# A hybrid S5 and GLA decoder layer: one over the root of every norm as exp(-ln/2) on ScalarE, in place of a mean and a reciprocal on VectorE and a square root between them

## The reference

```python
def rmsnorm(x, g):
    return x * lax.rsqrt(jnp.mean(x * x, axis=-1, keepdims=True) + EPS) * g

h = rmsnorm(x, g_mix);  z = h @ w_in          # u | q | k | v | r | a_low | gate_s5 | gate_gla
# S5: 32 groups, complex diagonal state x_t = A x_{t-1} + B u_t, y = Re(C x) + D u
z5 = gelu(y5);  o5 = z5 * sigmoid(z5 @ w_s5_glu)
# GLA: 4 heads, S_t = diag(alpha_t) S_{t-1} + k_t^T v_t, o_t = q_t S_t
og = og * lax.rsqrt(jnp.mean(og * og, axis=-1, keepdims=True) + EPS) * g_gla_norm    # per head, 128 wide
og = og * silu(r)
x = x + (sigmoid(gate_s5) * (o5 @ w_s5_br) + sigmoid(gate_gla) * (og @ w_gla_br)) @ w_out
x = x + jnp.square(relu(rmsnorm(x, g_ffn) @ w_ff1)) @ w_ff2
y = rmsnorm(x, g_final)
```

## Time and profile before

| | us |
|---|---|
| median of three runs | 3229.48 |
| lowest and highest | 3226.78 and 3229.75 |
| the profiled execution | 3223.25 |
| its span | 3221.4 |
| PE busy | 3006.3 (93%) |
| VectorE busy | 1452.4 (45%) |
| ScalarE busy | 505.0 (16%) |

### The profile page before, as it was taken

One profiled execution on the slowest core, in us unless ns is written; L12 is line 12 of the kernel. 1 busy time (PEld: TensorE's weight loads), 2 busy tenths in 40 slices (PEclk: granted clock), 3 DMA queues, 4 the chain that ended last, 5 costly groups with the idle time before them and its releaser, 6 DMA issues.

```text
span 3221.4 us, 46813 instructions
## 1 busy us (share of the span) xinstructions
PE 3006.3 (93%) x19116; PEld 2906.8 (90%) x19116; DVE 1452.4 (45%) x2573; ACT 505.0 (16%) x671; POOL 1161.5 (36%) x917
## 2 busy tenths in 40 slices
PE   4999997788999999999999999778999999999996
PEld 4899986688999999999999999667999999999996
DVE  7744536546353333333573353565445333333335
ACT  3221222141110000000122221213211000000001
POOL 3423321134444444444443323112444444443441
PEclk9989988899999999999999999788999999999998
DMA  3322323243111111111213222234121111111111
GB/s 123 103 93 67 74 83 91 85 150 92 47 43 47 49 44 49 44 49 47 96 51 115 66 68 67 86 97 165 60 76 44 49 47 47 46 46 47 46 46 68
DMA packets 115472, 226.59 MB, mean 70 GB/s; under 512 B 11824, under 2 KB 37200, under 8 KB 114128
## 3 DMA queue, kind: packets, MB, share of 16 engines
q1 hardware_dynamic: 65664, 119.57, 12.4%
q10 hardware_dynamic: 49616, 104.15, 10.0%
HBM read 181.71 MB, written 41.96 MB: 69 GB/s over the span
## 4 chain that ended last, share of the span: by engine, by line
PE 88%; DVE 8%; ACT 1%; issue 1%; DVEq 1%; DMA 1%; ACTq 1%
PE ps L456 27%; PE ps L457 26%; PE ps L458 26%; PE ps L598 2%; DVE f_g L1762 2%; DVE f_h L1353 1%; DVE r_o L1353 1%; PE ps L657 1%; PE ps L655 1%; DVE f_m L1353 1%; PE ps L677 1%; PE ps L678 1%; PE ps L692 1%; DVE f_o L1353 1%; DVE r_h L1353 1%
## 5 line engine op out<-in xcount | busy, mean ns | idle before, releaser
L438 POOL TENSOR_TENSOR w_hi<-w_raw,zero 128x512 fp32r<-128x512 f32 x456 | 524.2, 1150 | 1944.3 <-PE ps L458 1934.4
L456 PE MATMUL ps<-r_h,w_hi 128*128 128x344 f32 (+1 forms) x2736 | 896.9, 328 | 37.0 <-DVE r_h L1353 12.3
L458 PE MATMUL ps<-r_h,w_lo 128*128 128x344 f32 (+1 forms) x2736 | 881.7, 322 | 0.0
L457 PE MATMUL ps<-r_o,w_hi 128*128 128x352 f32 (+1 forms) x2280 | 736.7, 323 | 0.0
L440 POOL TENSOR_TENSOR w_lo<-w_raw,w_hi 128x512 fp32r<-128x512 f32 x456 | 640.0, 1403 | 64.7
L456 PE MATMUL ps<-r_z,w_hi 128*128 128x344 f32 (+1 forms) x1776 | 588.7, 331 | 27.1 <-DVE f_h L1353 15.6
L457 PE MATMUL ps<-r_h,w_hi 128*128 128x344 f32 (+1 forms) x1800 | 583.1, 324 | 0.0
L458 PE MATMUL ps<-r_z,w_lo 128*128 128x344 f32 (+1 forms) x1776 | 576.1, 324 | 0.0
L456 PEld LDWEIGHTS ps<-r_h,w_hi 128*128 128x128 f32 x2736 | 519.8, 190 | 49.7 <-issue 24.0
L458 PEld LDWEIGHTS ps<-r_h,w_lo 128*128 128x128 f32 x2736 | 519.6, 190 | 0.0
L457 PE MATMUL ps<-r_m,w_hi 128*128 128x344 f32 (+1 forms) x1392 | 448.2, 322 | 0.0
(11 more groups left out here) (336 smaller groups left out, 2860.2 us busy)
## 6 DMA issues: line engine op xcount, KB each, us to landing
w_raw<-wpack SPq DMA_DIRECT2D x456, 256.0 KB, 2.6
f_z<-s_constants ACTq DMA_DIRECT2D x16, 514.0 KB, 3.6
f_h<-s_constants ACTq DMA_DIRECT2D x16, 514.0 KB, 3.6
f_h<-xT ACTq DMA_DIRECT2D x4, 1040.0 KB, 9.5
gate_s_scratch<-f_o ACTq DMA_DIRECT2D x8, 520.0 KB, 3.3
f_h<-gate_s_scratch ACTq DMA_DIRECT2D x8, 520.0 KB, 14.1
f_h<-xT ACTq DMA_DIRECT2D x8, 520.0 KB, 3.5
f_o<-xT ACTq DMA_DIRECT2D x4, 1040.0 KB, 9.9
```

What stands on the lines that cost most here:

```text
L438: pool.tensor_tensor(w_hi[:, s, :], raw, zero[:, :].to_broadcast([P, WB]), ALU.subtract)
L456: pe.matmul(out, wh, h, start=first, stop=False)
L457: pe.matmul(out, wh, l, start=False, stop=False)
L458: return pe.matmul(out, wl, h, start=False, stop=last)
```

## The change

Every norm's root changes its form. Before: VectorE makes mean plus EPS from PSUM, ScalarE takes the square root, VectorE the reciprocal. After: ScalarE reads the sums from PSUM with Ln, with 1/n as the scale and a tile `eps` as the bias, and then takes Exp with scale -0.5 in place; VectorE waits for the result and scales. So PSUM is freed by ScalarE where it was freed by VectorE. The Ln of a head's part stands at the end of ScalarE's round in which PE makes the sum, behind the gate blocks; Exp follows the second Ln. Heads 2 and 3 have their sums a round earlier (6 and 8), all heads are scaled one round earlier against their sums, the small sample norm's Ln and Exp stand in round 0. The constant tile is set by VectorE before the tile of ones, and ScalarE waits for that before its first Exp.

```diff
-SAMPLE_MEAN = 1
-NORM_SUM = [1, 3, 7, 9]
+SAMPLE_SCALE = 2
+NORM_SUM = [1, 3, 6, 8]
...
+        eps = sb("eps", [P, 1])
...
             def norm_root(n, at):
-                act.wait_ge(ms_read, 3 * (n + 1))
-                act.activation(ft(at), ft(at), ACT.Sqrt).then_inc(std_ready, 1)
+                for b, (c0, cn) in enumerate(BLK):
+                    act.wait_ge(ms_done, 3 * n + b + 1)
+                    act.activation(ft(at)[:, c0:c0 + cn], ps[:, sum_bank(n, b), 0:cn], ACT.Ln, bias=eps[:, :],
+                                   scale=1.0 / D_MODEL).then_inc(ms_read, 1)
+                act.drain()
+                act.activation(ft(at), ft(at), ACT.Exp, scale=-0.5).then_inc(root_ready, 1)
+
+            def head_log(half, n, out, sums):
+                act.wait_ge(gms_done, half * NORM_PARTS + n + 1)
+                act.activation(out, sums, ACT.Ln, bias=eps[:, :], scale=1.0 / DV).then_inc(gms_read, 1)
+
+            def head_root(out):
+                act.drain()
+                act.activation(out, out, ACT.Exp, scale=-0.5).then_inc(groot_ready, 1)
...
-                    if t == SAMPLE_MEAN:
-                        act.wait_ge(gms_read, half * NORM_PARTS + 1)
-                        act.activation(fv(E_SQ, HEADS * DT), fv(E_SQ, HEADS * DT), ACT.Sqrt).then_inc(gstd_ready, 1)
+                    if t == 0:
+                        head_log(half, 0, fv(E_SQ, HEADS * DT), ps[:, 5, 0:HEADS * DT])
+                        head_root(fv(E_SQ, HEADS * DT))
                     for h in range(HEADS):
-                        if t == NORM_SUM[h] + 2:
-                            act.wait_ge(gms_read, half * NORM_PARTS + 2 * h + 3)
-                            g = ft(A_G, h % 2)[:, 0:TP]
-                            act.activation(g, g, ACT.Sqrt).then_inc(gstd_ready, 1)
+                        if t - NORM_SUM[h] in (0, 1):
+                            part = t - NORM_SUM[h]
+                            head_log(half, 2 * h + part + 1, ft(A_G, h % 2)[:, 512 * part:512 * (part + 1)], ps[:, 5, :])
+                            if part:
+                                head_root(ft(A_G, h % 2)[:, 0:TP])
...
             act.wait_ge(s5in_landed, 16)
+            act.wait_ge(ones_ready, 1)
...
             def norm_root(n, at):
-                for b, (c0, cn) in enumerate(BLK):
-                    dve.wait_ge(ms_done, 3 * n + b + 1)
-                    dve.tensor_scalar(ft(at)[:, c0:c0 + cn], ps[:, sum_bank(n, b), 0:cn], 1.0 / D_MODEL, EPS,
-                                      ALU.mult, ALU.add).then_inc(ms_read, 1)
-                dve.wait_ge(std_ready, n + 1)
-                dve.reciprocal(ft(at), ft(at))
-                dve.drain()
+                dve.wait_ge(root_ready, n + 1)
...
             def sample_scale(half):
-                dve.wait_ge(gstd_ready, half * (HEADS + 1) + 1)
+                dve.wait_ge(groot_ready, half * (HEADS + 1) + 1)
                 g = fv(E_SQ, HEADS * DT)
-                dve.reciprocal(g, g)
-                dve.drain()
...
-            def head_mean(half, h, part):
-                dve.wait_ge(gms_done, half * NORM_PARTS + 2 * h + part + 2)
-                dve.tensor_scalar(ft(A_G, h % 2)[:, 512 * part:512 * (part + 1)], ps[:, 5, :], 1.0 / DV, EPS,
-                                  ALU.mult, ALU.add).then_inc(gms_read, 1)
...
             def head_scale(half, h):
                 g = ft(A_G, h % 2)
-                dve.wait_ge(gstd_ready, half * (HEADS + 1) + h + 2)
-                dve.reciprocal(g[:, 0:TP], g[:, 0:TP])
-                dve.drain()
+                dve.wait_ge(groot_ready, half * (HEADS + 1) + h + 2)
...
                     s5_pair(half, t)
-                    if t == SAMPLE_MEAN:
-                        sample_mean(half)
-                    if t == SAMPLE_MEAN + 1:
+                    if t == SAMPLE_SCALE:
                         sample_scale(half)
                     for h in range(HEADS):
-                        if t - NORM_SUM[h] in (1, 2):
-                            head_mean(half, h, t - NORM_SUM[h] - 1)
-                        if t == NORM_SUM[h] + 3:
+                        if t == NORM_SUM[h] + 2:
                             head_scale(half, h)
...
+            dve.memset(eps[:, :], EPS)
             dve.memset(ones[:, :], 1.0).then_inc(ones_ready, 1)
```

More of the change, by code:

```diff
@@ L292, in build @@
         sq_ready, sq_used, ssum_ready, ms_done = sem("sq_ready"), sem("sq_used"), sem("ssum_ready"), sem("ms_done")
-        ms_read, std_ready = sem("ms_read"), sem("std_ready")
+        ms_read, root_ready = sem("ms_read"), sem("root_ready")
         full_ready, hi_ready, split_ready = sem("full_ready"), sem("hi_ready"), sem("split_ready")
@@ L315, in build @@
         silu_ready, osq_ready, gms_done = sem("silu_ready"), sem("osq_ready"), sem("gms_done")
-        gms_read, gstd_ready = sem("gms_read"), sem("gstd_ready")
+        gms_read, groot_ready = sem("gms_read"), sem("groot_ready")
         gs_stored = [sem("gs_stored0"), sem("gs_stored1")]
```

## The result

The changed kernel took 3178.18 us (median of four runs, 3175.85 to 3180.26), the kernel before 3229.61 beside it: a ratio of 0.9839, 95% interval 0.9822 to 0.9856, so 51 us faster. The forecast was 3181, with a range of 3156 to 3204. The profiled execution took 3175.85 with a span of 3174.1, 47.4 less than that of before.

What follows compares the result with a forecast made beforehand. It took PE's waits in the S5 loops, where head norms hold VectorE, as the bound; 37 us from the loops plus 10.8 at the ends made 48, so 3175 profiled and 3181 as median, range 3156 to 3204.

Steps and rivals of the forecast that it cites:

- Sum: Whole kernel: 37 us from the two S5 loops plus 10.8 from first and last norm, 48 saved.
- Prices: ScalarE's norm instructions: Ln 0.68 for 512 columns, 0.55 for 344, Exp 1.06 for 1024, two table loads of 1.28.
- Waits in a half: PE's norm-related waits in one S5 loop: 36.0 us before, 17.5 after, so 18.5 less per half.
- Clock: PE's granted clock in the S5 loops: no change taken; bounds per half 14 us won to 6 lost.
- waits of 10: PE's old single waits behind heads, 10.2 us at one followed; two per half, each losing 1.6 to the clock.
- double ones: PE waiting twice, to write the next pair's input and then for its rows; 5.3 us of clock lost each.
- Ends and inner norms: Full-width norms: the open first and last save 5.4 us each, 10.8 together; the four inner ones nothing.
- A shared table: Rival, every norm: Ln and Exp share one table load, 58 us won, 3171; chance 0.06.
- a longer path: Rival, ScalarE at the heads: each root some 3 us later, only 24 won, 3205; chance 0.14.
- the ends alone: Rival: only first and last norm pay, loop waits return elsewhere; 11 us won, 3218; chance 0.04.
- a bank freed too late by ScalarE: Rival, head sums' PSUM bank: ScalarE falls behind, PE waits every round; slower, 3246 at path 13; chance 0.03.
- The clock gain: Rival, S5 loops: PE's clock holds, up to 28 us beyond the 48, 3153; chance 0.20 together with shared table.

Runs made afterwards that it cites:

- e5_extra: Changed kernel plus a one-column square root between Ln and Exp of every norm, forcing a third table load per root; 3196.94 us.
- e9_again: The changed kernel run once more, unedited, on the chip of later follow-ups; 3178.61 us.
- e6_early: Changed kernel with ScalarE's head logs and roots moved ahead of the gate blocks, row stores and squares of their round; 3126.54 us.
- e1_full: Kernel before with only the six full-width norms in the new form, heads left old; 3222.2 us, ratio 0.9981.
- e10_old_early: Kernel before, old norm form and rounds, with only ScalarE's head square roots moved ahead of the gate blocks, stores and squares; 3167.03 us.
- e4_keep: Changed kernel with heads 2 and 3 put back to their old sum rounds, 7 and 9; 3183.81 us, ratio 0.9865.

## Why the prediction was right, and what it did not see

**Sum.** It said 48 for the profiled execution, which lost 47.4: 36.2 in the loops where 37 were forecast, 5.4 at either end as forecast, and small shifts of 1 to 2 in between that cancel (970.4 to 968.6 from the end of the second loop to the last row sums, 1369.2 to 1370.5 between the loops). That it came this close was in part luck. The 36.2 are 15.2 in half 0 and 21.0 in half 1, where 18.5 were forecast for each: the waits fell by 18.9 in both, but PE's busy time rose by 3.7 in the one and fell by 2.2 in the other. And both profiled executions had the stretch ahead of the first loop at the same pace (PE busy 417.8 and 417.7), where other executions have up to 426. The medians give 51.

**Prices.** Ln over 512 took 0.69 (0.68 forecast), over 344 0.55 (0.55), Exp over 1024 1.06 (1.06), and each root has two loads of 1.28, as forecast. From the evacuation's start to the scaling it is 501.25 - 495.92 = 5.3 at head 0, where 5.3 was the sum. The Trainium skill, ScalarE: Activation LUTs (Table sets; What ACT_TABLE_LOAD costs) has Ln and Exp in one set with one load, and adds a drain to each load: no run here shows either, as 498.86 is a second load and 496.82 + 1.28 = 498.10 meets the Ln at 498.11.

**Waits in a half, forecast and measured in half 0:** sample norm 0.7 and 0.85; head 0 0.4 and 0.31 (at the bank of the next sum, not at a pair); head 1 5.2 and 4.97; head 2 6.4 and 6.1; head 3 4.8 and 4.67; together 17.5 and 16.9. Of the 36.0 before, which it put behind heads, 2.3 stood elsewhere: 1.0 at the sample norm's mean and 1.3 at the rows of a pair (501.83), where no head was being scaled. The eight stores and the square ahead of head 2's second block were where the sum had them. e5_extra shows that the path itself is the cause: 1.5 more on it gave 5.2 to 6.6 more per half.

**Clock.** No change was taken for it, because waits of 10 would be replaced by double ones. PE's busy time in the loops went from 147.1 and 152.1 to 150.8 and 149.9, 1.5 more in all (e9_again has 148.6 and 148.2, 2.4 less). So no change was right within some 3 us, as a balance of two halves that went opposite ways. e6_early shows that the stake was real: 11 per half come back once the double waits go.

**Ends and inner norms.** e1_full's trace has the two ends at 5.4 each, and its 9 leave nothing for the inner norms.

**Rivals.** A shared table, a longer path, the ends alone and a bank freed too late by ScalarE: no trace shows one of them. The clock gain didn't come with this change.

**What it did not see.** It costed the root from the end of the gate block, before and after, and took that start as given. But in the kernel before VectorE had made head 0's last mean at 501.87 and stood idle for 8.71 ahead of the reciprocal, while the Sqrt stood in ScalarE's queue behind stores and two gate blocks (VectorE, then ScalarE):

```profile
501.87 0.69 DVE L1756 TENSOR_SCALAR f_g<-ps 128x512 f32<-128x512 f32 x1
```

```profile
504.49 3.96 ACTq L1127 DMA_DIRECT2D y_scratch<-f_o  x8
509.03 0.46 ACT L875 ACTIVATE f_o<-ps 128x352 f32<-128x352 f32 x1 [4.56 <-PE ps L458]
512.72 0.46 ACT L875 ACTIVATE f_o<-ps 128x344 f32<-128x344 f32 x1 [3.23 <-PE ps L458]
```

The slow reciprocal and the late place in the queue stood behind one another, and either could be taken away: of 36 us of waits per half the new form took 19, the early place alone 26 (e10_old_early), both together 35 (e6_early). The forecast of this change was not hurt, since the change keeps that place.

## What to carry to other kernels

When a slow step stands behind a wait, look at what is ahead of its producer in that producer's own queue before rewriting the step: here moving a few lines on ScalarE gave 62 us, rewriting the norm with its rounds 51, and both together 98 to 103. Time a path from the moment its input exists, not from the instruction that happens to stand before it. And waits of the matmul engine cost the clock as well: where 15 us of them per loop went, 11 more came back in matmuls.

## What the runs showed of the hardware

VectorE and GpSimd slow each other when they overlap. Over the first loop the same 340 instructions of VectorE and 28 of GpSimd were busy for 86.9 and 39.5 in e6_early and for 82.4 and 33.2 in e9_again; that overlaps make up all of this is not shown. Beside the rows of e4_keep, in e6_early a copy of 16 columns took 1.00 us where 0.17 is usual, and ended as GpSimd's instruction did (518.73 + 1.00 against 517.69 + 2.02). The Trainium skill, SBUF (SBUF: two separate sides), describes a port pair that the two share as an exclusive lock; these rows agree.

One program with the same waits ran the stretch ahead of its first loop 8.4 us longer in one execution than in another, by the granted clock: PE was busy for 426.4 and 417.7 with the same matmuls, and in the stage of 240 to 260 us the clock was 0.83 and 1.00.
